# The first projections of a two-block transformer kernel: context values from weights that are still held, rotations between projection halves, modulation units beside the Hyena projections

## The reference, cut to what matters

```python
mod_x = silu_c @ w_mod + b_mod              # 6 x 1024 columns; only the first 2 x 1024 are needed before hx
hx = modulate(rmsnorm(x, norm_mix), sh_a, sc_a)        # 1024 tokens
hc = modulate(rmsnorm(ctx, norm_mix), csh_a, csc_a)    # 256 context tokens
q_x, k_x, v_x, hy_x = split(hx @ w_in)      # 512 + 512 + 512 + 1536 columns
k_c, v_c = hc @ w_k, hc @ w_v
q_x, k_x = axial_rope(q_x), axial_rope(k_x)
attn = differential_attention(q_x, [k_c, k_x], [v_c, v_x])
hyo  = hyena(short_conv(hy_x))              # width-3 convolution along the tokens
x = x + g_a * (concat(attn, hyo) @ w_out)   # and then both FFNs and a second block
```

## Time and profile before

| what | us |
|---|---|
| median of 3 runs | 3388.32 (3386.03 to 3389.41) |
| the profiled execution | 3387.65 |
| its span in the trace | 3385.8 |
| PE busy, share of the span | 3189.8, 94% |
| step 1, `v` | 200.8 to 250.4 |
| step 2, `vc` | 250.4 to 270.1 |
| step 3, `qk` with the rotations, and the first `hy` | 270.1 to 409.05 |
| the other eleven `hy` | 409.05 to 532.6 |
| from there to DVE's first maximum of the attention | 532.6 to 556.9 |

### The profile page before, as it was taken

One profiled execution on the slowest core, in us unless ns is written; L12 is line 12 of the kernel. 1 busy time (PEld: TensorE's weight loads), 2 busy tenths in 40 slices (PEclk: granted clock), 3 DMA queues, 4 the chain that ended last, 5 costly groups with the idle time before them and its releaser, 6 DMA issues.

```text
span 3385.8 us, 37173 instructions
## 1 busy us (share of the span) xinstructions
PE 3189.8 (94%) x14552; PEld 2481.3 (73%) x14552; DVE 2233.1 (66%) x2747; ACT 1282.0 (38%) x1946; POOL 895.2 (26%) x858
## 2 busy tenths in 40 slices
PE   7898997998999899999999999998889989999999
PEld 3476785666777788888887888865557877888887
DVE  6654346886775987774448766587754599898433
ACT  5331113553223433333334333367531344444322
POOL 1111200224232143331100444413644124333101
PEclk9999998999999999999999999998899999999999
DMA  6434442002444222225434344541113422222643
GB/s 224 136 117 145 149 149 100 22 23 96 143 141 162 87 100 82 87 69 196 160 117 131 104 128 157 181 143 39 37 49 120 161 81 89 79 88 74 203 136 123
DMA packets 110952, 391.63 MB, mean 116 GB/s; under 512 B 14424, under 2 KB 17048, under 8 KB 110394
## 3 DMA queue, kind: packets, MB, share of 16 engines
q1 hardware_dynamic: 62122, 218.77, 20.2%
q0 software_dynamic: 48656, 170.49, 14.5%
HBM read 306.30 MB, written 82.90 MB: 115 GB/s over the span
## 4 chain that ended last, share of the span: by engine, by line
PE 62%; DVE 9%; issue 2%; ACT 2%; POOL 1%; DMA 0%; ACTq 0%; DVEq 0%; POOLq 0%
PE PS L370 19%; PE PS L371 19%; PE PS L372 19%; PE PS L3115 2%; PE PS L3076 2%; DVE HL L327 1%; PE PS L3098 1%; POOL Sc L3324 1%; DVE E L3250 1%; DVE QR L1486 1%; ACT HL L311 0%; PE PS L2738 0%; DVE HT L1867 0%; DVE kt L1502 0%; DVE kt L1504 0%
## 5 line engine op out<-in xcount | busy, mean ns | idle before, releaser
L370 PE MATMUL PS<-H,HL 128*128 128x512 f32 x1920 | 758.5, 395 | 27.2 <-DVE ko L693 12.1
L327 DVE TENSOR_TENSOR HL<-RAW,HL 128x1024 fp32r<-128x1024 f32 (+1 forms) x442 | 499.8, 1132 | 389.5 <-ACT HL L311 380.1
L371 PE MATMUL PS<-H,HL 128*128 128x512 f32 x1920 | 750.6, 391 | 0.0
L372 PE MATMUL PS<-H,HL 128*128 128x512 f32 x1920 | 750.3, 391 | 0.0
L311 ACT ACTIVATE HL<-RAW 128x1024 fp32r<-128x1024 f32 (+1 forms) x442 | 373.9, 847 | 919.7 <-PE PS L372 886.3
L370 PEld LDWEIGHTS PS<-H,HL 128*128 128x128 f32 x1920 | 362.3, 189 | 116.3 <-issue 31.2
L371 PEld LDWEIGHTS PS<-H,HL 128*128 128x128 f32 x1920 | 362.8, 189 | 76.0 <-issue 2.0
L372 PEld LDWEIGHTS PS<-H,HL 128*128 128x128 f32 x1920 | 362.5, 189 | 76.2
L370 PE MATMUL PS<-HT,HL 128*128 128x512 f32 x720 | 282.7, 393 | 17.9 <-DVE rows L2189 15.7
L371 PE MATMUL PS<-HT,HL 128*128 128x512 f32 x720 | 281.8, 391 | 0.0
L372 PE MATMUL PS<-HT,HL 128*128 128x512 f32 x720 | 281.6, 391 | 0.0
(11 more groups left out here) (392 smaller groups left out, 5226.1 us busy)
## 6 DMA issues: line engine op xcount, KB each, us to landing
RAW<-in_w_up SPq DMA_DIRECT2D x100, 512.0 KB, 3.6
RAW<-in_w_down SPq DMA_DIRECT2D x88, 512.0 KB, 3.6
RAW<-in_w_proj SPq DMA_DIRECT2D x48, 512.0 KB, 3.6
scr_hid<-hidr POOLq DMA_DIRECT2D x36, 512.0 KB, 2.9
HTf<-scr_hid POOLq DMA_DIRECT2D x72, 256.0 KB, 3.7
RAW<-in_w_wmodr SPq DMA_DIRECT2D x32, 512.0 KB, 4.5
RAW<-in_w_wout SPq DMA_DIRECT2D x26, 512.0 KB, 4.0
scr_res<-HTf POOLq DMA_DIRECT2D x48, 256.0 KB, 3.3
```

The lines of the kernel that those rows point to most:

```text
L327: e.tensor_tensor(lo, part_source(k, j, x)[0], hi.bitcast(F32), ALU.subtract).then_inc(*k.low.mark(j, x))
L370: e.matmul(out, lh, rh, start=first, stop=False)
L371: e.matmul(out, lh, rl, start=False, stop=False)
L372: return e.matmul(out, ll, rh, start=False, stop=last)
```

## The change

Four things. **(a)** `vc` uses the pairs of units 9, 10 and 11, which are still in `HL` after `v`, and only unit 8 is loaded and split again (last). No `wmodr` unit stands in step 2 any more. **(b)** The two halves of `rope(n-1)` stand behind the first and the second half of projection n; `rope(7)` stands between the halves of `hy` 0. **(c)** The `wmodr` units: one behind each of the eight `qk` units, then three behind each of `hy` 0 to 3, two behind each of 4 to 9, none behind 10 and 11, and none behind the last. `mod_sums` comes behind `hy` 0, 3, 6 and 10 (before: behind `hy` 0, `hy` 8, and two at the end). **(d)** The splits are placed by unit number (`k.qkv_units`) and no longer by a counter; one or two units are split ahead.

```diff
+def mods_at(n):
+    return 3 if n < 4 else 2 if n < 10 else 0
...
-    out += [("wqkv", i) for i in range(8, 12)]
-    for i in [*range(8, 12), *range(8)]:
+    out += [("wqkv", i) for i in [*range(8, 12), 8]]
+    for i in range(8):
         out += [("wqkv", i), rest.pop(0)]
     for i in range(12):
-        out += [("whyp", i), rest.pop(0)]
-    out += rest
+        out += [("whyp", i)] + [rest.pop(0) for _ in range(mods_at(i))]
...
-        k.used[j] = s.pe.at("v", u_)
+        k.used[j] = s.pe.at("v", 0) if u_ == 0 else s.pe.at("vc", u_ - 1)
+        held[u_] = uh, ul
...
-    for u_ in range(4):
-        j, uh, ul = take(k, e, "wqkv", 8 + u_)
+    for n, u_ in enumerate((1, 2, 3, 0)):
+        if u_ == 0:
+            j, *held[0] = take(k, e, "wqkv", 8)
+            k.used[j] = s.pe.at("vc", 3)
+        uh, ul = held[u_]
...
+    def projected(b, h, uh, ul):
+        claim(b + h)
+        for q in range(8):
+            x = mm3(e, PS[:, b + h, :], uh[:, blk(q)], ul[:, blk(q)], H[:, 0, q, blk(h, 512)], H[:, 1, q, blk(h, 512)], q == 0, q == 7)
+        return x
...
         for h in range(2):
-            claim(b + h)
-            for q in range(8):
-                x = mm3(e, PS[:, b + h, :], uh[:, blk(q)], ul[:, blk(q)], H[:, 0, q, blk(h, 512)], H[:, 1, q, blk(h, 512)], q == 0, q == 7)
-        x.then_inc(*s.pe.mark("qk", n))
+            x = projected(b, h, uh, ul)
+            if h:
+                x.then_inc(*s.pe.mark("qk", n))
+            if n:
+                rope(n - 1, h)
...
-        if n:
-            rope(n - 1)
-        one_mod(4 + n)
-    rope(7)
+        k.next_unit += 1
     for n in range(12):
...
+            if n == 0:
+                rope(7, h)
...
-        one_mod(12 + n)
-    for n in range(24, 32):
-        one_mod(n)
-    mod_sums()
+        k.next_unit += mods_at(n)
+        if n in (0, 3, 6, 10):
+            mod_sums()
...
+    mods = iter(range(8, 32))
     for n in range(12):
-        split_low(k, e, unit + 2)
-        unit += 1
+        split_low(k, e, units[14 + n])
+        if n == 0:
+            rope(7)
+        for _ in range(mods_at(n)):
+            mod(next(mods))
...
-        mod(12 + n)
-        split_low(k, e, unit + 2)
-        unit += 1
-    for n in range(24, 32):
-        mod(n)
-        unit += 1
-    split_low(k, e, unit + 1)
+    split_low(k, e, units[26])
```

More of the change, by code:

```diff
@@ L800, in mod_sums @@
         x.then_inc(*s.pe.mark("mod", gr))
-    def one_mod(n):
-        k.next_unit += 1
-        if n % 8 == 4 and n > 8:
-            mod_sums()
     free[6], free[7] = [k.start.act.at("mod", 1)], [k.start.dve.at("modc", 1)]
+    held = {}
     for u_ in range(4):
@@ L826, in pe_qkv, with rope @@
                 e.wait_ge(*s.dve.at("c_lo", kt))
[L827 to L832, removed]
+                x = mm3(e, PS[:, i, :], Hc[:, 0, kt, blk(i)], Hc[:, 1, kt, blk(i)], uh[:, blk(q, 512)], ul[:, blk(q, 512)], n == q == 0, n == 3 and q == 1)
+        x.then_inc(*s.pe.mark("vc", n))
     free[0], free[1] = [s.dve.at("vc")], [s.act.at("vc")]
-    def rope(n):
+    def rope(n, h):
         sl = k.slots_qkv["rope", n, 0][0]
@@ L838, in rope @@
         e.wait_ge(*s.act.at("rope", n))
[L839 to L842, removed]
+        claim(6)
+        e.matmul(PS[:, 6, :], k.perm[:, :], k.ev[:, sl, blk(h, 512)], start=True, stop=True).then_inc(*s.pe.mark("rope", n, h))
+        free[6] = [s.dve.at("rsin", n, h)]
+    def projected(b, h, uh, ul):
[3 more added lines that the diff above has]
+        return x
     for n in range(8):
@@ L869, in pe_qkv @@
         for h in range(2):
[L870 to L873, removed]
+            x = projected(b, h, uh, ul)
+            if h:
+                x.then_inc(*s.pe.mark("hy", n))
+            if n == 0:
+                rope(7, h)
         free[b] = free[b + 1] = [s.dve.at("hy", n, 1)]
         k.used[j] = s.pe.at("hy", n)
-        one_mod(12 + n)
-    for n in range(24, 32):
-        one_mod(n)
-    mod_sums()
+        k.next_unit += mods_at(n)
+        if n in (0, 3, 6, 10):
+            mod_sums()
     free[7] = [s.dve.at("modx")]
@@ L895, in act_qkv @@
         e.activation(Hc[:, 0, i, :], k.xc[:, i, :], ACT.Identity, bias=k.modc[:, i:i + 1]).then_inc(*s.act.mark("c_hi", i))
-    unit = 32
-    for u_ in range(4):
-        split_high(k, e, unit + 3)
-        unit += 1
+    units = k.qkv_units
+    split_high(k, e, units[3])
     e.wait_ge(*s.dve.at("c_lo", 7))
@@ L904, in act_qkv @@
         e.activation(k.ev[:, sl, 512:1024], PS[:, i + 1, :], ACT.Copy).then_inc(*s.act.mark("v", i))
-    for u_ in range(4):
-        split_high(k, e, unit + 4)
-        unit += 2
+    split_high(k, e, units[6])
     e.wait_ge(*s.pe.at("vc", 3))
@@ L910, in act_qkv @@
     for n in range(8):
-        split_high(k, e, unit + 3)
-        unit += 1
+        split_high(k, e, units[min(7 + n, 13)])
         sl = k.slots_qkv["rope", n, 0][0]
@@ L917, in act_qkv @@
         e.activation(k.ev[:, sl, :], k.two(P["qk", n]), ACT.Copy, scale=0.125 if n < 4 else 1.0).then_inc(*s.act.mark("rope", n))
-        split_high(k, e, unit + 3)
-        unit += 1
     cb, cw = SOFF["hy_conv_b"], SOFF["hy_conv_w"]
     for n in range(12):
-        split_high(k, e, unit + 3)
-        unit += 1
+        split_high(k, e, units[14 + n])
         ev_free(k, e, ("hy", n))
@@ L927, in act_qkv @@
         e.activation(o, k.two(P["hy", n]), ACT.Identity, bias=k.small[:, cb + n:cb + n + 1], scale=k.small[:, cw + 12 + n:cw + 13 + n]).then_inc(*s.act.mark("hy", n))
-        split_high(k, e, unit + 3)
-        unit += 1
-    split_high(k, e, unit + 8 + 2)
+    split_high(k, e, units[27])
 def dve_qkv(k, e):
@@ L961, in dve_qkv @@
             c_low(i - 1)
-    unit = 32
-    for u_ in range(4):
-        split_low(k, e, unit + 2)
-        unit += 1
+    units = k.qkv_units
+    split_low(k, e, units[3])
     e.wait_ge(*s.pe.at("v", 3))
@@ L986, in mod @@
         k.used[j] = s.dve.at("mod", n)
-    for u_ in range(4):
-        split_low(k, e, unit + 2)
[L990 to L993, removed]
+    split_low(k, e, units[6])
     e.wait_ge(*s.pe.at("vc", 3))
@@ L1008, in dve_qkv @@
     for n in range(8):
-        split_low(k, e, unit + 2)
-        unit += 1
+        split_low(k, e, units[min(7 + n, 13)])
+        mod(n)
         if n:
@@ L1108, in sp_qkv @@
 def sp_qkv(k, e):
-    load_weights(k, e, 37)
+    load_weights(k, e, k.qkv_units[5])
     after(e, *k.start.every(), *k.st_ko)
@@ L3636, in build @@
         k.tables = [j for j, name in enumerate(names) if name in ("fcos", "fsin")]
+        k.qkv_units = [j for j, name in enumerate(names) if name in ("wqkv", "whyp", "dfwd")][:28]
         k.first_rest = [j for j, name in enumerate(names) if name == "wmodr"]
```

1 line of the change is left out of this document (added).

## The result

| | before | after |
|---|---|---|
| median, us | 3388.51 (3386.03 to 3389.41, 4 runs) | 3364.39 (3361.96 to 3366.68, 4 runs) |
| profiled execution, its span | 3387.65, 3385.8 | 3361.96, 3360.1 |
| context values (`vc`) | 18.9 | 11.0 |
| from there to the end of `hy` 0, rotations included | 138.91 | 123.85 |
| from there to the end of `hy` 11 | 123.45 | 137.44 |

The ratio after/before is 0.993, 95% interval 0.9916 to 0.9944: faster by 0.7%, 24.1 us between the medians. Between the two profiled executions the first maximum comes 26.1 earlier (530.78 against 556.86 in the earlier trace rows) and the end of the span 25.7 earlier, so what is won in this stage reaches the end.

A forecast was written before the change was run, and what follows sets the result against it. PE, busy 94% of the span, was taken as the bound, its standstills as what could be won. 8.0 + 14.3 - 3.7 - 5.5 + 16.3 = 29.4 saved gave 3358.9 us; 3350 to 3368 held 8 in 10.

The forecast's parts named there:

- the main case: Whole kernel: waits in the Hyena stretch cost between 2 and 9 us, all else as counted; 3355 to 3363, chance 0.52.
- (a) Context values: Context values step: no wait for a late low part, 10.9 us instead of 18.9; 8.0 us saved.
- (b) Rotations: Rotations among the projections: sixteen halves at 0.92 us instead of about 29 in all; 14.3 us saved.
- E: Time mark in the forecast: the end of the last key projection's 48 matmuls, from which the Hyena stretch was followed.
- (c) Two column sums: Hyena stretch: two column sums of 1.84 us move in from its end; 3.7 us lost there.
- (c) Waits: Hyena stretch: PE waits for late `whyp` loads, with some matmuls at the lower clock; 5.5 us lost (0 to 12).
- For `whyp` 3 the ring gives 12.2: Hyena stretch: the buffer cycle takes 12.2 us with 6.0 for landing, against PE's 10.9, so PE waits 1.3.
- The end: Last projection to the attention's first maximum: no modulation units or column sums left there; 16.3 us saved (14 to 18).
- T+8: Forecast first maximum, 8 us after the last projection ends, released by the last store landing at T+7.8.
- The ring dominates: Rival, Hyena stretch: every landing in three-unit turns takes 8.1 us, 20 lost instead of 5.5; 3373 us, chance 0.13.
- The ring keeps up: Rival, Hyena stretch: a `whyp` load behind three others lands within 4.6 us, cycle below 10.88; 3352 to 3354, chance 0.22.
- The rule weighed: Load landings in the Hyena stretch: fixed 2.0 us plus bytes at 436 GB/s; no waits, an estimate of 3353 us.

The follow-up runs named there:

- its own experiment: Changed kernel with both rotation halves put back behind the projection and the last two together behind the last one: 3368.84 us, ratio 0.9944.
- whyp first: Changed kernel with each `whyp` unit listed ahead of the modulation units of the turn before: 3350.07 us, ratio 0.9891.
- heads late, units ahead: Changed kernel with head loads behind the store of `hy` 9 and modulation units 8 to 10 ahead of DVE's last rotation: 3349.03 us, ratio 0.9886.
- the reloading kernel: Changed kernel with all four value units loaded and split again for the context values, no modulation unit between them: 3368.86 us, ratio 0.9934.
- the heads late: Changed kernel with the first two attention heads' loads issued behind the store of `hy` 9: 3357.49 us, ratio 0.9908.
- the units ahead of the rotation: Changed kernel with modulation units 8 to 10 ahead of DVE's work for the last rotation: 3356.19 us, ratio 0.9901.

## Why the prediction was right, and where it was off

The time was forecast at 3359 and is 3364.39. That is outside the 3355 to 3363 of the main case, which had 0.52 and wanted at most 9 lost to waits, and inside the 3350 to 3368 given 8 in 10. The profiled executions' difference was forecast at 29.4 and is 25.7. By the steps:

- **(a) Context values, 8.0:** 7.9 (18.9 to 11.0). The wait and its cause were read rightly from the earlier trace rows. But the reason given, that three of the four units are there already, is not what does it: reloading all of them without modulation units is as fast, and with them 8.9 slower.
- **(b) Rotations, 14.3:** 15.1 in the profile, 15.2 in its own experiment. The halves cost 0.90 (they stand 6.34 apart, 5.44 of it half a projection). Before, they cost 29.6 in all, above the 29 taken: 138.91 less nine projections of 10.88 and four context keys of 2.86, which is how much further apart the halves of after stand where a context key lies between them. The price of this part on DVE was in the numbers and was not seen: the text has `whyp` 2 issued at E+22.1, behind DVE's last rotation (E+22.4 measured, with E at 369.15), but never asks what would start sooner if the units stood ahead of that rotation.
- **(c) Two column sums, 3.7:** 3.7.
- **(c) Waits, 5.5: this is the term that was off most, by 4.8.** The third stretch takes 137.44. Eleven projections at 10.88 and four sums of 1.84 are 127.0, so 10.4 are lost, and 0.1 by the same count before: 1.46 and 6.65 as waits, 1.7 in `hy` 3 at the lower clock level (417.73 to 430.32 is 12.6 for 10.9), 0.3 in `hy` 2. The forecast had 3.2 ahead of `hy` 2, 1.3 ahead of `hy` 3, and 1. The sentence "here I take 8.1" put the collision with the head loads on `whyp` 2; that load is issued 1.7 before them and landed in 5.9. The full burst falls on `whyp` 3, 10.8. "For `whyp` 3 the ring gives 12.2" is what failed: from ACT to ACT it takes 17.9, the landing of 10.8 for 6.0 and 7.0 for the 6.2 of the rest. Even without the head loads the turns take 13.7 (6.7 to land, 7.0 for the rest) and 13.5 (7.5 and 6.0).
- **The end, 16.3:** 16.6. T+7.8 for T+8, but the scores release the maximum and not the store; the two were forecast 0.3 apart. In the run with whyp first it is the store, at T+7.4.
- **Outside the sum:** the context values start 0.5 earlier for no reason of this change, 0.4 of the gain is not seen at the end of the span, and the median lies 2.4 above the profiled execution, not 0.7. Together: 4.8 for the waits, 0.1 for (a), 0.4 at the end of the span and 1.7 for the median, less 0.8 for (b), 0.3 for the end of the stage and 0.5 for the earlier start. That is 5.4, from 3359 to 3364.4.

*The ring dominates* was the rival nearest to what happened, with half of its 20 lost, but not in its manner: one turn loses most, not four alike. *The ring keeps up* was not seen: with the head loads gone and DVE early nothing waits, but the turns still take 12.6, and it is the lead that hides them. The rule weighed gave 3.9 from issue to landing for the fourth of four loads. The Trainium skill ("DMA: Bandwidth & Descriptors", Anatomy of one DMA) fits one transfer by itself. No `whyp` load here that was issued within 4 us of the first of its three companions landed in less than 5.2; with no head load in flight such loads took 5.2 (heads late, units ahead) to 8.2 (after, the load for `hy` 4). The measurement decides.

Three things make the waits, each of which was taken away by itself: the order in the ring (all of the 10.3 gone), DVE held up in `rope(7)` (6.2), and the head loads (5.0). They don't add up like that: the first alone brings what the last two bring together, since either way the load for the next projection is there before PE asks. Between medians the versions without waits are 12.5 to 15.4 faster than after, though the stage explains 10.3. The intervals are some 5 us to either side, so the rest is not explained and may be none.

## What to carry to other kernels

Where a load that the bound engine needs and loads that only spare time needs share one ring in order, put the needed one first: here this alone won back the 10.3 us of the stage, for which the head loads and the held-up DVE could also be blamed, and made landings of 6 to 9 us harmless. Where work is spread into a stretch, follow the ring's length from measured landings with as many loads in flight as there will be, and place a burst of other transfers by the time of its issue: here it hurt the load issued behind it (10.8 to land), not the one 1.7 ahead of it (5.9, with the burst and without). And when an instruction is moved to fill a gap on one engine, ask what is queued behind its partner on the other: here DVE stood before its half of the moved rotation with three units queued behind, and the loads of the next stretch started late.

## What was not expected of the hardware

The granted clock falls in one execution and stays up in another behind the same work. In the Hyena stage behind the attention, which no edit touches, after and the reloading kernel have the same wait of 1.78 for the same instruction (PE at 993.81 and at 995.96). The clock stays at 1.00 in both for the ten microseconds behind it. Then, behind the same sixteen small matmuls (1001.32 and 1003.47, 2.05 us), after falls to 0.50 from about 1004.6 to 1008, and the other does not fall until 1012.2 at least. The windows that hold this stretch have 0.83 and 1.00:

```profile
1000.00:1010.00 10.00, 10.00 (x45) 8.05 (x44) 7.38 (x11) 4.36 (x7) 3.81 (x3) 0.83 0.01 2
...
1002.20:1012.20 10.00, 10.00 (x52) 8.21 (x52) 7.41 (x11) 4.41 (x7) 3.88 (x3) 1.00 0.01 2
```

Ten microseconds at 0.83 are 1.7 lost. Such pieces come and go: from the end of `hy` 11 to the first matmul of the feed-forward stage on `HT` it is 598.7 in after and 595.6 in the reloading kernel. Ahead of the stage, the first projection of v starts at 200.4 to 201.2 in nine of the twelve changed kernels' profiles and at 204.25 to 204.41 in the other three. Neither goes with an edit. Nor does the length of a wait alone decide: the 2.52 ahead of `hy` 3 with the heads late was followed by a window at 1.00, while the 0.90 ahead of `hy` 4 with the units ahead of the rotation was followed by one at 0.78. That shorter wait stood right behind a column sum (425.33, 1.84 us of one-column matmuls); whether the sum had a part in it is not shown. The windows of these two kernels:

```profile
410.00:415.00 5.00, 2.48 (x12) 1.73 (x11) 2.38 (x2) 2.15 (x2) 0.00 (x0) 1.00 0.13 53
415.00:420.00 5.00, 5.00 (x24) 4.14 (x23) 4.47 (x5) 0.00 (x0) 0.10 (x1) 1.00 0.67 213
...
430.00:435.00 5.00, 5.00 (x18) 4.04 (x18) 4.36 (x4) 0.00 (x0) 0.21 (x1) 0.78 0.89 252
```

That is why a stretch was compared here by its own start and end, and why 3 us between the spans of two profiles say nothing by themselves.
